# Norm weights, half products, a split load and merged routing steps in a hybrid encoder layer

## The reference

```python
h = rms_norm(x, attn_norm_g)
proj = h @ w_in          # GDN q|k|v 1536, z 512, alpha 4, beta 4, SWA q 512, k 128, v 128
y_a = gated_delta_rule(conv4+silu(q,k,v), decay, beta), gated rms_norm    # 4 heads of 128
y_b = sliding-window attention, 8 q / 2 kv heads of 64, window 128, sinks
x = x + concat(y_a, y_b) @ w_out
h = rms_norm(x, ffn_norm_g)
x = x + sum over the top 2 of 4 experts in the top group of 4:
        gate * (silu(h @ Wg) * (h @ Wu)) @ Wd                             # 16 experts, 256 wide
```

## Time and profile before

| | us |
|---|---|
| median of three runs | 980.98 |
| profiled execution, in all | 977.75 |
| its span | 975.9 |
| TensorE busy | 927.5 (95%) |
| VectorE busy | 593.3 (61%) |
| ScalarE busy | 234.6 (24%) |
| GpSimd busy | 217.0 (22%) |
| mean granted TensorE clock | 0.995 |

### The profile page before, as it was taken

How to read it: one execution, slowest core, us unless ns; L and a number is a source line. 1 busy time by engine, 2 the same in 40 slices (tenths; PEclk the granted TensorE clock), 3 DMA queues, 4 the chain that set the end, 5 groups by cost and what they waited for, 6 DMA issues and landing times.

```text
span 975.9 us, 19077 instructions
## 1 busy us (share of the span) xinstructions
PE 927.5 (95%) x7577; PEld 681.8 (70%) x7577; DVE 593.3 (61%) x1812; ACT 234.6 (24%) x606; POOL 217.0 (22%) x302
## 2 busy tenths in 40 slices
PE   5999999999999999999999998889999999999995
PEld 5787687596686868769769676565667666777663
DVE  2366775784685687487578468988534324345443
ACT  1233331431431342234143233231010111111010
POOL 7020020020011002002002000400244454465653
PEclk9999999999999999999999999999999999999998
DMA  8920101020010110110100002812557976979621
GB/s 305 395 91 1 45 22 45 1 66 22 23 66 1 45 45 22 44 36 32 44 2 23 21 24 71 339 67 66 179 171 238 343 232 215 346 260 357 219 91 57
DMA packets 51491, 113.99 MB, mean 117 GB/s; under 512 B 11191, under 2 KB 14519, under 8 KB 51392
## 3 DMA queue, kind: packets, MB, share of 16 engines
q1 hardware_dynamic: 35072, 87.07, 24.9%
q0 software_dynamic: 14592, 25.22, 7.7%
q10 hardware_dynamic: 1728, 0.31, 0.2%
HBM read 112.54 MB, written 25.17 MB: 141 GB/s over the span
## 4 chain that ended last, share of the span: by engine, by line
PE 78%; DVE 16%; DMA 2%; issue 2%; ACT 1%; SPq 0%; POOL 0%; POOLq 0%; DVEq 0%; ACTq 0%
PE pm L417 71%; PE pm L420 6%; DVE pqkv L1405 4%; DMA w_sb<-in_w_in 2%; DVE X L1558 1%; DVE bs L1623 1%; DVE sc L1628 1%; DVE xT L1344 1%; DVE hT L1360 1%; PE pm L798 1%; DMA qkvT<-h_mid,w_sb 0%; DVE V_S L1636 0%; DVE xT L1223 0%; ACT pqkv L978 0%; DVE y_mix L1649 0%
## 5 line engine op out<-in xcount | busy, mean ns | idle before, releaser
L417 PEld LDWEIGHTS pm<-hT,w_sb 128*128 128x128 f32 x1544 | 177.0, 194 | 9.5 <-DVE hT L1360 6.0
L417 PE MATMUL pm<-hT,w_sb 128*128 128x128 f32 x1544 | 178.9, 278 | 4.9 <-DVE hT L1360 4.3
L417 PE MATMUL pm<-w_sb,hT 128*128 128x512 f32 (+1 forms) x384 | 148.1, 534 | 0.4 <-DMA w_sb<-in_w_in 0.4
L1918 POOL TENSOR_TENSOR tail<-tail,rows 128x512 f32<-128x512 f32 x8 | 10.2, 1269 | 511.4 <-ACT aTm L999 511.4
L417 PE MATMUL pm<-wo_sb,pT 128*128 128x512 f32 x256 | 115.0, 596 | 2.8 <-ACT pT L1046 2.1
L417 PEld LDWEIGHTS pm<-w_sb,hT 128*128 128x128 f32 x384 | 70.7, 191 | 57.1 <-issue 52.9
L417 PE MATMUL pm<-ctmp,w_sb 128*128 128x128 f32 x768 | 88.8, 276 | 1.1 <-DVE ctmp L1706 1.1
L1405 DVE SCALAR_TENSOR_TENSOR pqkv<-ci,cw,pqkv 128x128 f32<-128x128 f32 x288 | 77.6, 344 | 19.9 <-ACT pqkv L978 19.6
L417 PEld LDWEIGHTS pm<-ctmp,w_sb 128*128 128x128 f32 x768 | 86.7, 192 | 2.6 <-issue 2.0
L417 PEld LDWEIGHTS pm<-wo_sb,pT 128*128 128x128 f32 x256 | 46.7, 190 | 53.0 <-issue 49.3
L1778 DVE TENSOR_TENSOR ci<-pm,gain 128x512 f32<-128x512 f32 x32 | 20.6, 686 | 82.6 <-PE pm L798 48.7
(11 more groups left out here) (315 smaller groups left out, 1527.0 us busy)
## 6 DMA issues: line engine op xcount, KB each, us to landing
w_sb<-in_w_gate_up SPq DMA_DIRECT2D x12, 2048.0 KB, 14.8
w_sb<-in_w_down SPq DMA_DIRECT2D x12, 1024.0 KB, 6.5
w_sb<-in_w_in SPq DMA_DIRECT2D x4, 2048.0 KB, 20.5
wo_sb<-in_w_gate_up SPq DMA_DIRECT2D x4, 2048.0 KB, 14.6
xt<-in_x SPq DMA_DIRECT2D x8, 512.0 KB, 4.4
xT<-in_x_turned SPq DMA_DIRECT2D x8, 512.0 KB, 3.5
wo_sb<-in_w_out SPq DMA_DIRECT2D x1, 4096.0 KB, 21.8
sc<-in_x SPq DMA_DIRECT2D x8, 512.0 KB, 3.5
```

What stands on the lines that cost most here:

```text
L417: return pe.matmul(o_, lhsT=l_, rhs=r_, start=start, stop=stop, skip_group_check=True)
L1918: g.tensor_tensor(qk_in[:, 0:QH, :], qk_in[:, 0:QH, :], gqk[:, None, 0:DH].broadcast_to([P, QH, DH]), ALU.mult)
```

## The change

- In tiles 1 to 5 `gain_x(nn)` moves from level 2 to ahead of `add_x(0)`.
- `gate_inputs` moves from after the levels to ahead of tap 3 at level 5; ScalarE's `gates` stands ahead of the copy of chunk 5 in all tiles.
- The row factors are spread into bank 2, after the `v0` product (at the start: ahead of chunk 5), the diagonal lies in another tile of SBUF, and the first chunk's products begin with the first half of `hT`; the second half is waited for at k = 4.
- `rsqrt_one` forms the rsqrt of one column in 10 steps instead of 12. It is used in `row_factors` and in `Late.factor`.
- Chunk 1 of `w_in` is loaded in two halves of 256 columns, as chunk 0 is.
- Routing: the steps for the two picks are merged into one on both, the counts' products are reordered around the wait, each one-hot pair signals for itself, the row numbers are taken from PSUM ahead of the table's copy, fewer filler products are issued.
- In the first expert `turn_halves` stands ahead of `sum_gates`; the half-gate products and the table's copy come later.

The core of the diff:

```diff
                 c0, n = CHUNKS[c]
-                if c == 0:
+                if c < 2:
                     n //= 2
-                    sp.dma_start(w_sb[:, :, 0:n], w_in[0, :, 0:n].rearrange("(k p) n -> p k n", p=P)).then_inc(half_w_loaded, 16)
-                    c0 = n
+                    sp.dma_start(w_sb[:, :, c0:c0 + n],
+                                 w_in[0, :, c0:c0 + n].rearrange("(k p) n -> p k n", p=P)).then_inc(half_w_loaded[c], 16)
+                    c0 += n
                 sp.dma_start(w_sb[:, :, c0:c0 + n],
                              w_in[0, :, c0:c0 + n].rearrange("(k p) n -> p k n", p=P)).then_inc(w_loaded[c], 16)
...
                 pe.wait_ge(F.rstd_ready, t + 1)
-                if later(t):
-                    pe.wait_ge(F.chunk_copied, 6 * t - 1)
-                mm(spread_bank(t)[:, 0:P], ones[:, :], rstd_diag).then_inc(F.rstd_spread, 1)
+                mm(pm[2][:, 0:P], ones[:, :], rstd_diag).then_inc(F.rstd_spread, 1)
 
             def project(t, c, ks=range(KD)):
 
                 c0, n = CHUNKS[c]
                 if ks[0] == 0:
                     if c < 2:
-                        pe.wait_ge(F.hT_ready, 2 * t + 2 if c or later(t) else 1)
-                        if c and later(t):
-                            pe.wait_ge(F.chunk_copied, 6 * t)
+                        pe.wait_ge(F.hT_ready, 2 * t + 1 + c)
+                        if later(t):
+                            pe.wait_ge(F.chunk_copied, 6 * t - 1 + c)
                     else:
                         pe.wait_ge(F.chunk_copied, 6 * t + c - 1)
                     if isinstance(t, int) and t == 0:
-                        pe.wait_ge(w_loaded[c] if c else half_w_loaded, 16)
+                        pe.wait_ge(half_w_loaded[c] if c < 2 else w_loaded[c], 16)
                 if c < 3:
                     for h in range(H):
-                        if c == t == 0 and h == H // 2:
+                        if c < 2 and t == 0 and h == H // 2:
                             pe.wait_ge(w_loaded[c], 16)
                         for k in ks:
-                            if c == t == h == 0 and k == KD // 2:
-                                pe.wait_ge(F.hT_ready, 2)
+                            if c == h == 0 and k == KD // 2:
+                                pe.wait_ge(F.hT_ready, 2 * t + 2)
                             ins = mm(pm[BANK[c]][:, h * P:(h + 1) * P], w_sb[:, k, c0 + h * P:c0 + (h + 1) * P], hT[:, k, :],
                                      k == 0, k == KD - 1)
                 else:
@@ -466,9 +465,11 @@
                 project(t, 0)
 
             def front(t):
-                for c in range(1, NC_):
+                for c in range(1, NC_ - 1):
                     project(t, c)
-                start(1)
+                spread_rstd(1)
+                project(t, NC_ - 1)
+                project(1, 0)
...
                 ins.then_inc(B.v0_done, 1)
+                if nn is not None:
+                    spread_rstd(nn)
                 ahead(5, range(4, KD))
...
             keep_busy(pm[3], 3)
+            pe.wait_ge(A.rank_ready, 1)
+            mm(pm[1][:, 0:n], ones[:, :], before, True, False)
             pe.wait_ge(R.picks, 1)
-            pe.wait_ge(A.rank_ready, 1)
-            mm(pm[1][:, 0:n], upper_strict, picks[:, AHEAD * NE:], True, False)
             for t in range(AHEAD, NT - 1):
                 mm(pm[1][:, (t + 1 - AHEAD) * NE:n], ones[:, :], both_picks[:, t:t + 1].rearrange("p t g e -> p t (g e)")
                    .broadcast_to([P, NT - 1 - t, NE]), False, False)
-            mm(pm[1][:, 0:n], ones[:, :], before, False, True).then_inc(R.counts, 1)
+            mm(pm[1][:, 0:n], upper_strict, picks[:, AHEAD * NE:], False, True).then_inc(R.counts, 1)
             for t in range(AHEAD, NT):
                 mm(pm[7][:, 0:NE], ones[:, :], picks[:, t * NE:(t + 1) * NE], t == AHEAD, False)
             mm(pm[7][:, 0:NE], ones[:, :], cum[:, AHEAD, :], False, True).then_inc(R.counts, 1)
             late_hots = [c * NT + t for c in range(TOPK) for t in range(AHEAD, NT)]
-            keep_busy(pm[3], 4)
-            pe.wait_ge(R.hots, 1)
-            for u in late_hots:
+            keep_busy(pm[3], 2)
+            for i, u in enumerate(late_hots):
+                pe.wait_ge(R.hots, i + 1)
                 ins = mm(pm[0][:, 0:P], hot_mod[u], hot_row[u], False, u == late_hots[-1])
             ins.then_inc(R.rows_summed, 1)
             keep_busy(pm[3], 1)
-            pe.wait_ge(R.rows_ready, 1)
+            pe.wait_ge(R.rows_ready, 2)
...
+            def sum_half_gates():
                 pe.wait_ge(R.table_ready, 1)
...
-            keep_busy(pm[3], 2)
+            keep_busy(pm[3], 1)
             turn_rows(0)
             keep_busy(pm[3], 1)
             for i in range(NE + 1):
                 if i < NE:
                     gate_up(i)
+                if i < NE:
+                    turn_halves(i)
                 if i == 0:
                     sum_gates()
-                if i < NE:
-                    turn_halves(i)
                 if i == NE:
                     down(i - 1, 0)
                     down(i - 1, 1)
@@ -934,6 +937,8 @@
                     down_half(i - 1, 1)
                     down(i - 1, 0)
                 gate_up_halves(i)
+                if i == 0:
+                    sum_half_gates()
...
+                if nx is not None:
+                    gates(nx)
+                ahead(5)
                 if t == NT - 2:
-                    ahead(5)
-                    gates(nx)
                     copy_yb(t)
-                else:
-                    if nx is not None:
-                        gates(nx)
-                    ahead(5)
...
+            def rsqrt_one(step, y, a, tmp, src, scale):
+
+
+                step(v.tensor_scalar(a, src, scale, EPS, ALU.mult, ALU.add))
+                step(v.tensor_scalar(y.bitcast(I32), a.bitcast(I32), 1, None, ALU.logical_shift_right))
+                step(v.tensor_scalar(y.bitcast(I32), y.bitcast(I32), -1, RSQRT_MAGIC, ALU.mult, ALU.add))
+                for c in (1, -2):
+                    step(v.scalar_tensor_tensor(tmp, y, a, y, ALU.mult, ALU.mult))
+                    step(v.scalar_tensor_tensor(y, tmp, -3.0 * c * c, y, ALU.add, ALU.mult))
+                c = 16
+                step(v.scalar_tensor_tensor(tmp, y, a, y, ALU.mult, ALU.mult))
+                step(v.tensor_scalar(tmp, tmp, -0.5 / c ** 3, 1.5 / c, ALU.mult, ALU.add))
+                step(v.tensor_tensor(y, tmp, y, ALU.mult))
+
...
             def route_rows(t0, n, ranks):
 
                 ts = slice(t0, t0 + n)
-                for c, pick in enumerate((pick1, pick2)):
-                    tt(prod[:, ts], pick[:, ts], ranks.rearrange("p t (g e) -> p t g e", g=GROUPS), ALU.mult)
-                    route_step(v.tensor_reduce(rank_of[:, c, ts], prod[:, ts].rearrange("p t g e -> p t (g e)"), AX_X,
-                                               ALU.add))
+                tt(prod_of[:, :, ts], picks_of[:, :, ts], ranks.unsqueeze(1).broadcast_to([P, TOPK, n, NE]), ALU.mult)
+                route_step(v.tensor_reduce(rank_of[:, :, ts], prod_of[:, :, ts], AX_X, ALU.add))
                 tt(past_ranks[:, :, ts], over_last(rank_of[:, :, ts], RANKS),
                    steps_f.unsqueeze(1).unsqueeze(1).broadcast_to([P, TOPK, n, RANKS]), ALU.is_ge)
                 route_step(v.tensor_reduce(comb_of[:, :, ts], past_ranks[:, :, ts], AX_X, ALU.add))
-                for c in range(TOPK):
-                    route_step(v.scalar_tensor_tensor(mod_of[:, c, ts], comb_of[:, c, ts], -float(P), rank_of[:, c, ts],
-                                                      ALU.mult, ALU.add))
-                    route_step(v.scalar_tensor_tensor(comb_of[:, c, ts], comb_of[:, c, ts], float(NE), expert_of[:, c, ts],
-                                                      ALU.mult, ALU.add))
+                route_step(v.scalar_tensor_tensor(mod_of[:, :, ts], comb_of[:, :, ts], -float(P), rank_of[:, :, ts],
+                                                  ALU.mult, ALU.add))
+                route_step(v.scalar_tensor_tensor(comb_of[:, :, ts], comb_of[:, :, ts], float(NE), expert_of[:, :, ts],
+                                                  ALU.mult, ALU.add))
...
+                if nn and pv:
+                    nn.gain_x()
...
+                    if l == 5 and nx:
+                        nx.gate_inputs()
...
-                    if l == 2 and nn:
+                    if l == 2 and nn and not pv:
...
-                    ins = row_hots(c, t)
-            ins.then_inc(R.hots, 1)
+                    row_hots(c, t).then_inc(R.hots, 1)
             v.wait_ge(R.rows_summed, 1)
-            step(v.tensor_copy(table[:, 0, :], pm[0][:, 0:P]))
-            rows_of(table[:, 0, 0:NE], NE, slot_rows).then_inc(R.rows_ready, 1)
+            rows_of(pm[0][:, 0:NE], NE, slot_rows).then_inc(R.rows_ready, 1)
```

(29 more changed lines are left out.)

28 lines of the change are left out of this document (10 added, 18 removed).

## The result

The changed kernel takes 967.88 us (median of 4 runs, 967.41 to 968.34), the kernel before on the same chip 980.47 (978.22 to 981.66): 0.9875 of it, 95% interval 0.9858 to 0.9891. In a second comparison it was 966.82 against 979.21, ratio 0.9885 (0.9868 to 0.9903). The profiled execution took 967.41 us (span 965.7), 10.3 less than that of before.

What follows compares the result with a forecast made beforehand. TensorE was taken to bound the kernel (78% of the chain), so only its waits can be won. Terms -2.3 -1.8 -0.9 -0.8 -1.5 -1.2 +1.2 = -7.3 us gave 970.4 against the profile, 973.7 as median; range 970.0 to 977.6.

Steps and rivals of the forecast that it cites:

- the second chunk's loads: Start of the kernel: 1 KB rows slow the load stream, tile 1's projection starts later; 1.2 us lost.
- the rate of packets: SP queue at the start: beside ACT's small loads it stays at 178 packets a us, so 0.75 MB less is moved.
- rival (a): Start: the load stream keeps its rate, the front gains 0.6 us; in all -9.1, 971.8 us; chance 0.22.
- The shorter root: Row factors: two fewer steps save 0.39 us, on the chain in tile 7 and once after it; 0.8 us gained.
- The halves of hT: Next tile's projection starts on the first half of hT, removing TensorE's 0.30 us wait; six tiles, 1.8 us gained.
- The norm weights: Tiles 1 to 5: the earlier multiply removes 0.46 of TensorE's 0.50 us wait before level 4; 2.3 us gained.
- Gate inputs: Tile 6: earlier gate inputs remove VectorE's 1.00 us wait for the exponentials and TensorE's 0.87 for qkvT; 0.9 us gained.
- first expert: Half rows turned ahead of the gate sums: TensorE's waits of 0.39 and 0.80 us go; 1.2 us gained.
- Routing: After the tiles: merged and reordered steps save 2.2 us, less 0.7 at the first gather; net 1.5 us gained.
- the collision of 0.7: First gather: starting earlier, it shares the engines with a 1 MB weight load at half rate; 0.7 us lost.
- Rival (b): Clock falls in new places, before chunk 2 and around the first gather; one or two falls, 975.3 to 977.1 us; chance 0.17.
- (d): Slower: repeated clock falls at 1.7 us each, five give 982.2 us; waits under 1.6 us had left the clock alone; chance 0.03.

## Why the prediction was wrong, point by point

**The term that failed: the second chunk's loads, +1.2 on record, -1.73 measured, 2.9 us.** The step that failed is the rate of packets: that 1 KB rows beside the small loads stay at 178 packets a us, so that 0.75 MB less are moved and chunk 3 starts 2.0 us later. In the changed kernel q1 moved 302 packets a us beside 224 of q10, where it had 177 of 2 KB before. From 14 to 18 us it moved 1.24 MB in rows of 1 KB and 1.36 MB before, 0.12 less and not 0.75 (0.24 less in its second execution), and chunk 3 landed no later than before. The low rate at 12 to 13 us, from which the limit was read, is there in the changed kernel too and is over at 14 (at 15 in the second), still in rows of 1 KB (12:13 and 14:15 us):

```profile
q1 hardware_dynamic: 196, 0.19, 66.9%
```
```profile
q1 hardware_dynamic: 301, 0.31, 91.5%
```

So most of the low rate belongs to that stretch of the start and not to the size of the row; what holds q1 down there was not looked into. The Trainium skill (DMA: Bandwidth & Descriptors, Specifications), by which transfers of 512 B and more run at line rate, agrees with the landings, 35.66 us on average with rows of 1 KB and 35.95 with 2 KB. This is rival (a), which had a chance of 0.22.

That accounts for 2.0 of the 2.9 us. Another 1.0 is luck: chunk 3 landed at 36.4 in the profiled execution of before and at 35.4 in that of the changed kernel, and both lie within the scatter of 35.0 to 36.5. What follows came out nearly as on record: the wait before tile 1 shrank from 1.53 to 0.85, for 0.7 on record, and is 1.42 with the split alone. The shorter root, which starts the first product 0.41 sooner in this execution (10.40 against 10.81), moves nothing behind it, since chunk 3 is waited for.

The prediction also says that behind chunk 1's wait stands only the load stream. This holds in the profiled execution of before, by 0.43 us. With the chunk whole, chunk 3's products start at the later of its landing and chunk 1's landing plus some 14.4 us; in three further executions it was the second (35.69, 36.83, 36.98), 0.2 to 1.2 us behind the load. The split takes that branch away, which is worth some 0.4 us on average (0.57 less 0.13, an estimate from the sixteen executions).

**The halves of hT: 0.30 a tile on record, 0.56 measured.** Right mechanism, term too small. The step that failed is to take the idle time shown as the cost of a wait. In tiles 0 to 5 this made some 1.4 us of the surplus. **The norm weights: 0.46 on record, 0.44 measured.** Here the same reading was right: next late was TensorE's own work, as said. Together 1.00 a tile.

**Gate inputs (-0.9) and first expert (-1.2)** came out at -0.97 and -1.28; the experiments gave 0.88 for the first and 0.60 + 0.68 for the second. **Routing** gave -2.19 with one root: the steps were worth 1.99 up to the gather (11.01 to 9.02 us behind the load) for 2.2 on record, and the collision of 0.7 did not take place. **The shorter root** was worth 0.20 in tile 7 (55.56 before, 55.36 in an execution without a fall there) instead of 0.39, and as much in the routing. The step that failed is the price of a step, 0.19 each: ten steps take 2.06 us (667.59 to 669.65) where twelve took 2.27, because three of those left take 0.22 where the ones in their place took 0.16.

**The clock.** Rival (b) had the price right and, for the changed kernel, the places wrong: none of the new waits at the start made it fall, nor those around the gather in its two traces; the old ones did, in some executions. Behind tile 0's wait of 1.94 it fell in 7 of the 13 executions that have this wait bare, behind tile 7's of 1.57 in 9 of 13, behind that of 1.01 in tile 7 in 2 of 15, once in the routing, and twice around the gather (with fillers, and in the wait of 4.59). A fall costs 1.7 us in tile 0 (67.88 against 66.20), 1.6 in tile 7 at the first wait, 2.4 at the other. In the two profiled executions before had one and after two, so the traces understate the change by one fall: -10.2 becomes -11.8. The argument against (d), that waits under 1.6 us leave the clock alone, is refuted by the nine falls behind the wait of 1.57.

**From the profiled execution to the median.** Against the profile the forecast was 970.4 for a measured 967.41, 3.0 off. The other 2.8 came from carrying over the 3.2 us by which before's median stood above its profiled execution. The changed kernel has no such distance (967.88 and 967.41). One fall less in before's profiled execution than in its usual one would explain 1.7 of it; this was not seen. So rival (a), with its 971.8, had the load stream right, and the time lies 3.9 below it: by this 2.8, by the halves, by the landing of chunk 3, less the fall in tile 7.

So the sum of the misses against the profile is: start -2.9, tiles -1.4, routing -0.3, tile 7 +1.8 (a fall, 1.6, and the root, 0.2), the rest -0.1; in all -2.9.

## What to carry to other kernels

A rate read in one short stretch is not yet a limit: ask whether the same stretch has it with the other row size as well. Where two waits stand in a row before a matrix engine, a load and the engine's own backlog, write the start as the later of two times and ask for both branches; an edit that is worthless on the branch seen can be worth 1 us on the other, which the next execution may take. A wait of 0.3 us between two groups of back-to-back products cost 0.55. And before a single execution is the base of a sum, look for falls of the clock in it: each was worth 0.17% here. What removes the wait removes both costs; filler removes the fall, and costs time itself where it is longer than the wait.

## What the runs showed of the hardware

In one and the same kernel the same wait, behind the same work, is followed by a fall of the granted clock from 1.00 to 0.50 in one execution and not in another: in the changed kernel's first it ended at 102.41 us (1.95 long) and the clock fell, in the second at 102.96 (1.94) and it stayed. What tells the two apart is not settled. The second runs 0.55 us later from the start, by its load stream, but the time of the wait alone does not order the executions: the clock fell where it ended at 102.61 and at 102.66, and stayed where it ended at 102.64. The falls in tile 0 and behind the wait of 1.57 in tile 7 lasted between 3 and 4 us; the two behind the wait of 1.01, where small products with short waits between them follow, about 7.

A gather of 128 rows took 4.6 us with nothing beside it and 8.1 inside a stream of weights (404 GB/s in all from 678 to 684 us), but 4.6 also when the stream ended 2 us into it (4.8 in the changed kernel's second execution).
